# Layer 1's attention on VectorE: the maxima of the scores before the step's weight split, the reciprocal of the sums before the branch read

## The chip, the cores and the metric

The kernel runs on one core of a Trainium2 chip. The metric is the device time of one execution in microseconds. Before the change it is 1315.0 us, the median of three runs (1313.83 to 1315.97).

## The reference

A two-layer diffusion backbone in fp32 for 256 latent and 256 context tokens of width 1024. Each layer normalises and modulates the tokens and projects them once; the columns of that projection feed an attention, a convolution branch (31 taps over positions), a short gated convolution and a Fourier branch, and four gates. Each branch is projected to 1024 channels, multiplied by its sigmoid gate, summed and projected again; a gated MLP follows. In layer 1 only the 256 latent tokens go through the branches. Its attention, cut to what matters:

```
s = q @ k.T * 64 ** -0.5          # 256 latent queries, 512 keys (own and context), 8 heads, band mask
m = maximum(max(s), sink)
p = exp(s - m)
y = (p / (sum(p) + exp(sink - m))) @ v
```

## The kernel before

**Weights in two halves.** Every fp32 product is made of three matmuls: w_hi with the high part of the data, w_hi with its low part, w_lo with its high part (L516 to L518, in `product`). Weights stream through four raw buffers. For each step, ScalarE copies the raw weights of the step three ahead to w_hi (`head`, L940) and VectorE subtracts to get w_lo (`rest`, L1227). A raw buffer is loaded again when VectorE's split of it is done. TensorE begins a step when the split of its weights is done.

**Places.** In layer 1 the eight "fn" steps are places 0 to 7, the eight "sc" steps places 8 to 15, and the first "at" steps go on from 16. A step of a place computes a gate (24 matmuls of 128x256 from h) and a mix (6 matmuls from the branch's data); VectorE's branch read (L1537, which signals `evac`) multiplies the two.

**The attention between the steps.** It is cut into eight batches (two query blocks, four pairs of heads). Batch k begins at place 2k, so it takes a pair of places. Helpers say what falls where: `at_place(layer, place, late)` gives the batch of an even offset, `halves_at` the batch and the half.

- TensorE, at place 2k, between the gate and the mix: the scores of batch k (L758 and the band mask, L764), after both exponentials of batch k-1 (they share the score banks); the values of batch k-2 (L786); the transposes of batch k-1's first half (L774). At place 2k+1: the transposes of its second half.
- VectorE: `peak(k)` at place 2k (two reductions to maxima, L1484, and two operations on two columns, L1487 and L1490); `attended_rest(k-2)` at place 2k (L1504); `weight_sum(k)` at place 2k+1 (the sum, L1496, and its reciprocal, L1498).
- ScalarE: `weigh(k, half)`, the exponential, at places 2k and 2k+1 (L1064); `share(k)`, both halves scaled by the reciprocal, at the start of place 2k+2 (L1075), ahead of that place's `head`; `turned`, the copy of the transposed weights, at places 2k+2 and 2k+3 (L1083).

**The order on each engine** is the order in which its program is written; all waiting is by semaphores. In a place, ScalarE runs share, head, the gate's tanh (L1118), attended, turned, weigh. VectorE runs `rest`, a conv tap (L1471), `peak` (even places), `attended_rest`, a second conv tap, the branch read, and then `weight_sum` (odd places). GpSimd runs the conv taps of the other channel half on its own (L478 and L480, until 978.8 us) and later the sums of the branches (L486).

`early_table` (L945) is a one-column activation into a scratch column, by which ScalarE loads its next function table early; the scratch column is a column of `small`, in which the maxima of even batches are kept.

Of the kernel before, what the change touches and what calls it, by code (L numbers as in the profile page):

```python
# [160 lines left out]
def program(nc, io):  # L161
    ctx = ExitStack()
    with ctx:
# [3 lines left out]
        def at(name, shape, dt, offset):  # L167
            return nc.alloc_sbuf_tensor_at(name, [P] + shape, dt, offset=offset)

        def place(name, shape, dt=F32):  # L170
            size = 4
            for s in shape:
                size *= s
            offset = top[0]
            top[0] += -(-size // 32) * 32
            return at(name, shape, dt, offset)
# [37 lines left out]
        small = place("small", [2, 6, 2])  # L214
        band = at("band", [3, P], BF16, top[0])
        top[0] += 2 * 3 * P
        root_col = place("root_col", [NT // P])
        ada_part = place("ada_part", [2, P * KD // 32])
        assert top[0] <= nc.sbuf_usable_end, (top[0], nc.sbuf_usable_end)

# [32 lines left out]
        def mix_bank(layer, n):  # L253
            return psB[1] if layer and n % 2 else psB[3]
# [4 lines left out]
        def score_bank(layer, half):  # L259
            return psA[2 - 2 * layer + half]  # L260
# [40 lines left out]
        def V(name, i):  # L301
            return vec[:, VEC[name] + i:VEC[name] + i + 1]
# [15 lines left out]
        def branch_sum(layer, o):  # L318

            return X[:, o, 0:NT] if layer == 0 else X[:, o, SEQ:NT]  # L320
# [22 lines left out]
        def at_place(layer, place, late):  # L343

            count, every = NB[layer], 1 + layer
            k, odd = divmod(place - late, every)
            return k if odd == 0 and 0 <= k < count else None
# [11 lines left out]
        def wide(layer, k):  # L359

            return (4 if batches(layer)[k][0] == 0 else 2) * P
# [568 lines left out]
        def _(act):  # L930
# [13 lines left out]

            def early_table(func):  # L945

                act.activation(small[:, 0, 0, 0:1], V("one", 0), func)

            def square(count, o, T, direct, before):

# [268 lines left out]
        def _(dve):  # L1219
            def rest(st, tiles):  # L1220

                if st.i is None and st.n + AHEAD >= TOTAL:
                    return
                s = (st.n + AHEAD) % SLOTS
                r, _ = st.filled("w", AHEAD)
                dve.wait_ge(head_done, st.up(st.n + AHEAD + 1))
                dve.tensor_tensor(w_lo[:, s, 0:tiles * P], raw[:, r, 0:tiles * P],  # L1227
                                  w_hi[:, s, 0:tiles * P].bitcast(F32), ALU.subtract).then_inc(rest_done, 1)

            def size(st, name):  # L1230
                return SIZE[START[name]] if st.i is not None else SIZE[(st.n + AHEAD) % PER_LAYER]
# [162 lines left out]
            for layer in range(DEPTH):  # L1394
# [67 lines left out]
                def conv_tap(j):  # L1462

                    w = V("conf_w", TAPS * layer + j)
                    src, dst = glu[:, 0, 0:S, j:j + SEQ], both(acc[:, 0, 0:T], T)
                    if j == 0:
                        dve.wait_ge(evac, n0 + LEN["in"])
                        op = dve.tensor_scalar(dst, src, w, V("conf_b", 2 * layer), ALU.mult, ALU.add)
                    else:
                        dve.wait_ge(tap, CONF_K * layer + j)  # L1470
                        op = dve.scalar_tensor_tensor(dst, src, w, dst, ALU.mult, ALU.add)  # L1471
                    op.then_inc(tap, 1)
# [4 lines left out]
                def peak(k):  # L1477
                    _, _, t = un[k]
                    b = b0 + k
                    sm = small[:, b % 2, :, :]  # L1480
                    sink = nsink[:, layer * N_HEADS + t:layer * N_HEADS + t + 5:4]
                    for half in range(2):
                        dve.wait_ge(s_mm, 2 * b + half + 1)
                        dve.tensor_reduce(sm[:, 0, half:half + 1], score_bank(layer, half)[:, 0:wide(layer, k)], AX.X,  # L1484
                                          ALU.max).then_inc(negm, 1)
                    dve.wait_ge(negm, 4 * b + 2)
                    dve.scalar_tensor_tensor(sm[:, 1, :], sm[:, 0, :], -HEAD ** -0.5, sink, ALU.mult, ALU.min)\  # L1487
                        .then_inc(negm, 1)
                    dve.wait_ge(negm, 4 * b + 3)
                    dve.tensor_tensor(sm[:, 5, :], sm[:, 1, :], sink, ALU.subtract).then_inc(negm, 1)  # L1490

                def weight_sum(k):
                    b = b0 + k
                    sm = small[:, b % 2, :, :]
                    dve.wait_ge(expd, 3 * b + 3)
                    dve.tensor_tensor(sm[:, 4, :], sm[:, 2, :], sm[:, 3, :], ALU.add).then_inc(den, 1)  # L1496
                    dve.wait_ge(den, 2 * b + 1)
                    dve.reciprocal(sm[:, 4, :], sm[:, 4, :]).then_inc(den, 1)  # L1498

                def attended_rest(k):  # L1500
                    s, qi, t = un[k]
                    c0 = SEQ * s + P * qi
                    dve.wait_ge(o_head, b0 + k + 1)
                    dve.tensor_tensor(y_lo[:, 4 + t, c0:c0 + P], out_bank[:, 0:P],  # L1504
                                      y_hi[:, 4 + t, c0:c0 + P].bitcast(F32), ALU.subtract).then_inc(o_rest, 1)

                def branch(name, b, place=None):
                    def step(st):
                        rest(st, size(st, name))
                        if name == "cf" and st.idx > 0:  # L1510
                            merged_rest(st.idx - 1)
                        o = st.idx
                        if place is not None:
                            if 2 * place < CONF_K:
                                conv_tap(2 * place)
                            k = at_place(layer, place, 0)
                            if k is not None:
                                peak(k)
                            k = at_place(layer, place, LATE[layer]["value"])
                            if k is not None:  # L1520
                                attended_rest(k)
                            if 2 * place + 1 < CONF_K:
                                conv_tap(2 * place + 1)
                            if layer == 0:
                                weight_sum(place)
                        dve.wait_ge(sigd, 34 * layer + 2 + 8 * b + o + 1)
                        dve.wait_ge(chunk_done, st.n + 1)
                        sg = (sig if b == 3 else gsig)[st.n % 2][:, 0:T]
                        ps = (psB[st.n % 2] if b == 3 else mix_bank(layer, st.n))[:, 0:T]
                        if b == 0:  # L1530
                            t = branch_sum(layer, o)
                        else:
                            t = (tmp if b == 3 else gtmp)[st.n % 2][:, 0:T]
                            g = 8 * (b - 1) + o
                            if g >= 2:
                                dve.wait_ge(m_sum, 24 * layer + g - (o > 0))
                        dve.scalar_tensor_tensor(t, sg, 1.0, ps, ALU.add, ALU.mult).then_inc(evac, 1)  # L1537
                        if place is not None and layer and place % 2:
                            weight_sum(place // 2)
                        if name == "fn" and o in (5, 6):  # L1540
                            c = o - 5
                            dve.wait_ge(sc_head, 2 * layer + c + 1)
                            dve.tensor_tensor(y_lo[:, 2 + c, 0:T], pc[:, c, 0:T],
                                              y_hi[:, 2 + c, 0:T].bitcast(F32), ALU.subtract).then_inc(sc_rest, 1)
                        if layer == 0:
                            ada_behind(st)
                    return step

                def merged_rest(o):
                    dve.wait_ge(m_head, 8 * layer + o + 1)  # L1550
                    dve.scalar_tensor_tensor(mg_lo[:, o, 0:T], branch_sum(layer, o), 0.5,
                                             mg_hi[:, o, 0:T].bitcast(F32), ALU.mult, ALU.subtract).then_inc(m_rest, 1)
# [6 lines left out]
                for idx in range(LEN["at"]):  # L1559
# [3 lines left out]
                    k = at_place(layer, 16 + idx, LATE[layer]["value"])  # L1563
# [244 lines left out]
```

## Time and profile before

| | |
|---|---|
| median of three runs | 1315.0 us |
| the profiled execution | 1315.8 us, its span 1314.0 us |
| TensorE busy | 1264.8 us, 96% of the span |
| VectorE busy | 885.3 us, 67% |
| ScalarE busy | 550.2 us, 42% |
| GpSimd busy | 292.9 us, 22% |
| granted TensorE clock, mean | 0.990 |
| layer 1's places 0 to 18 | 928 to 1022 us of the span, about |

Shares are of the span from the first to the last instruction. Busy time of an engine counts its instructions; time in which it waits for a semaphore is idle. In a row of the timeline the number in brackets is the idle time of the engine just before the instruction, and the arrow names what ended it.

### The profile page before, as it was taken

To read this page: it belongs to the slowest core of one execution; us is meant where nothing else is said; L and a number is where in the kernel's file an instruction comes from. 1 tells how busy PE (TensorE), PEld (TensorE's weight loads), DVE (VectorE), ACT (ScalarE), POOL (GpSimd) and SP (SyncE) were. 2 spreads that over 40 slices of the span, in tenths; PEclk is the share of its full clock that TensorE was granted. 3 is DMA by queue.
4 is the path that set the end of the run, shared out by engine and by line. 5 is a ranking of instruction groups with operands and counts; after the bars stand their busy time and mean duration, and the time that the engine had idled before them with its cause. 6 is when DMAs were issued, how large, how long until landed. Compare 5 with 4: busy or idle time off the path is not lost.

```text
span 1314.0 us, 19888 instructions
## 1 busy us (share of the span) xinstructions
PE 1264.8 (96%) x7661; PEld 1094.7 (83%) x7661; DVE 885.3 (67%) x1203; ACT 550.2 (42%) x870; POOL 292.9 (22%) x247
## 2 busy tenths in 40 slices
PE   5999999999999999999999999999989998999997
PEld 3788777777788788888888888889878998999997
DVE  4698678652799767662889674476676667665654
ACT  4322355554423344331223332244556545653543
POOL 0003699110233001111001110003771130210210
PEclk9999999999999999999999999999999998999999
DMA  9465311212366415562646664135333554664561
GB/s 372 159 221 199 120 61 62 73 64 81 116 201 228 131 62 177 192 216 77 204 161 196 198 214 131 62 113 179 106 117 98 183 171 129 193 221 136 185 209 33
DMA packets 50339, 198.76 MB, mean 151 GB/s; under 512 B 5584, under 2 KB 6992, under 8 KB 49104
## 3 DMA queue, kind: packets, MB, share of 16 engines
q1 hardware_dynamic: 50256, 197.62, 45.4%
q8 instruction: 56, 0.92, 0.3%
q14 instruction: 27, 0.22, 0.1%
HBM read 196.55 MB, written 1.05 MB: 150 GB/s over the span
## 4 chain that ended last, share of the span: by engine, by line
PE 85%; DVE 9%; ACT 4%; issue 2%; DMA 1%; SPq 0%; ACTq 0%; DVEq 0%
PE psA L516 25%; PE psA L517 24%; PE psA L518 24%; DVE w_lo L1227 2%; ACT w_hi L940 2%; PE psB L518 2%; PE psB L516 2%; PE psB L517 2%; DVE acc L1471 2%; DVE small L1484 1%; PE psA L758 1%; PE psB L786 1%; PE psB L774 1%; PE psB L689 1%; PE psB L537 1%
## 5 line engine op out<-in xcount | busy, mean ns | idle before, releaser
L516 PE MATMUL psA<-h_hi,w_hi 128*128 128x256 f32 (+1 forms) x1544 | 525.4, 340 | 10.6 <-DVE h_lo L1347 4.9
L517 PE MATMUL psA<-h_lo,w_hi 128*128 128x256 f32 (+1 forms) x1544 | 518.3, 336 | 0.0
L518 PE MATMUL psA<-h_hi,w_lo 128*128 128x256 f32 (+1 forms) x1544 | 518.1, 336 | 0.0
L1227 DVE TENSOR_TENSOR w_lo<-raw,w_hi 128x1024 fp32r<-128x1024 f32 (+2 forms) x244 | 336.5, 1379 | 123.2 <-ACT w_hi L940 123.0
L940 ACT ACTIVATE w_hi<-raw 128x1024 fp32r<-128x1024 f32 (+2 forms) x244 | 277.0, 1138 | 303.1 <-PE psA L518 239.7
L516 PEld LDWEIGHTS psA<-h_hi,w_hi 128*128 128x128 f32 x1544 | 296.8, 192 | 44.4 <-issue 9.5
L518 PEld LDWEIGHTS psA<-h_hi,w_lo 128*128 128x128 f32 x1544 | 296.9, 192 | 29.1
L517 PEld LDWEIGHTS psA<-h_lo,w_hi 128*128 128x128 f32 x1544 | 297.1, 192 | 27.9 <-issue 0.2
L505 POOL TENSOR_TENSOR hid_lo<-sig,hid_hi 128x512 f32 (+3 forms) x44 | 67.7, 1539 | 477.6 <-ACT hid_hi L1191 477.6
L1248 DVE SCALAR_TENSOR_TENSOR ada_sum<-raw,csil,ada_sum 128x1024 f32<-128x1024 f32 x112 | 156.0, 1424 | 0.0
L516 PE MATMUL psA<-hid_hi,w_hi 128*128 128x256 f32 (+1 forms) x352 | 117.5, 334 | 2.1 <-DVE sig L1668 2.0
L518 PE MATMUL psA<-hid_hi,w_lo 128*128 128x256 f32 (+1 forms) x352 | 117.2, 333 | 0.0
L517 PE MATMUL psA<-hid_lo,w_hi 128*128 128x256 f32 (+1 forms) x352 | 117.1, 333 | 0.0
L1632 DVE SCALAR_TENSOR_TENSOR X<-psA,mod,X 128x256 f32<-128x256 f32 x55 | 25.2, 482 | 84.8 <-PE psA L518 84.8
L1658 DVE SCALAR_TENSOR_TENSOR tmp<-psA,vec,tmp 128x510 f32<-128x510 f32 (+1 forms) x44 | 27.1, 616 | 73.1 <-ACT tmp L1202 73.0
L480 POOL TENSOR_TENSOR acc<-acc,sqb 128x512 f32<-128x512 f32 (+1 forms) x60 | 75.1, 1252 | 5.0
L1202 ACT ACTIVATE tmp<-psA,vec 128x512 f32<-128x512 f32 (+1 forms) x44 | 29.5, 671 | 110.4 <-PE psA L518 110.4
L516 PEld LDWEIGHTS psA<-hid_hi,w_hi 128*128 128x128 f32 x352 | 66.8, 190 | 9.3 <-DVE w_lo L1227 2.9
L518 PEld LDWEIGHTS psA<-hid_hi,w_lo 128*128 128x128 f32 x352 | 66.9, 190 | 6.4
L517 PEld LDWEIGHTS psA<-hid_lo,w_hi 128*128 128x128 f32 x352 | 66.9, 190 | 6.4
L486 POOL TENSOR_TENSOR X<-X,tmp 128x512 f32<-128x512 f32 (+1 forms) x28 | 44.5, 1596 | 100.3 <-DVE tmp L1537 52.8
L486 POOL TENSOR_TENSOR X<-X,gtmp 128x512 f32<-128x512 f32 (+1 forms) x20 | 21.2, 1066 | 138.0 <-DVE gtmp L1537 93.8
(190 smaller groups left out, 1461.3 us busy)
## 6 DMA issues: line engine op xcount, KB each, us to landing
raw<-w_up SPq DMA_DIRECT2D x88, 512.0 KB, 4.3
raw<-w_ada SPq DMA_DIRECT2D x80, 512.0 KB, 3.6
raw<-w_dn SPq DMA_DIRECT2D x32, 704.0 KB, 4.8
raw<-w_in SPq DMA_DIRECT2D x36, 512.0 KB, 4.3
raw<-w_at SPq DMA_DIRECT2D x24, 512.0 KB, 3.5
raw<-w_fn SPq DMA_DIRECT2D x16, 640.0 KB, 3.9
raw<-w_sc SPq DMA_DIRECT2D x16, 640.0 KB, 3.8
raw<-w_cf SPq DMA_DIRECT2D x16, 640.0 KB, 3.9
```

Source lines behind the costliest of these rows:

```text
L480: pool.tensor_tensor(dst, dst, part, ALU.add).then_inc(tap_pool, 1)
L486: pool.tensor_tensor(dst, dst, src[:, 0:T], ALU.add).then_inc(m_sum, 1)
L505: pool.tensor_tensor(dst, sig[b][:, 0:T], src.bitcast(F32), ALU.subtract)\
L516: pe.matmul(out, w0, hi, start=first, stop=False)
L517: pe.matmul(out, w0, lo, start=False, stop=False)
L518: return pe.matmul(out, w1, hi, start=False, stop=last)
L940: act.activation(w_hi[:, s, 0:tiles * P], raw[:, r, 0:tiles * P], ACT.Copy).then_inc(head_done, 1)
L1202: act.activation(tmp[b][:, 0:T], psA[st.slot][:, 0:T], ACT.Identity, bias=Vd("ffn_b", st.up(p0 + pair, 2)), scale=Vd("ffn_w", st.up(3 * (p ...
L1227: dve.tensor_tensor(w_lo[:, s, 0:tiles * P], raw[:, r, 0:tiles * P], w_hi[:, s, 0:tiles * P].bitcast(F32), ALU.subtract).then_inc(rest_don ...
L1248: op = dve.scalar_tensor_tensor(dst, w, c, dst, ALU.mult, ALU.add)
L1471: op = dve.scalar_tensor_tensor(dst, src, w, dst, ALU.mult, ALU.add)
L1658: dve.scalar_tensor_tensor(t3[:, :, 1:SEQ], p3[:, :, 0:SEQ - 1], Vd("ffn_w", st.up(w, 6)), t3[:, :, 1:SEQ], ALU.mult, ALU.add).then_inc(cv, 1)
```

## The change

For layer 1 alone, two calls move within VectorE's order of a place. `peak(k)` goes from behind the first conv tap to the very start of the place, ahead of `rest`. `weight_sum` goes from behind the branch read to between the two conv taps. Layer 0 keeps its order. The scratch column that `early_table` writes becomes a tile of its own, `spare`, because the maxima of the first batch may now be taken at an earlier point. No instruction is added or removed.

```diff
+        spare = place("spare", [1])
...
-                act.activation(small[:, 0, 0, 0:1], V("one", 0), func)
+                act.activation(spare[:, 0:1], V("one", 0), func)
...
                 def branch(name, b, place=None):
                     def step(st):
+                        k = at_place(layer, place, 0) if place is not None else None
+                        if k is not None and layer:
+                            peak(k)
                         rest(st, size(st, name))
...
                             if 2 * place < CONF_K:
                                 conv_tap(2 * place)
-                            k = at_place(layer, place, 0)
-                            if k is not None:
+                            if k is not None and layer == 0:
                                 peak(k)
                             k = at_place(layer, place, LATE[layer]["value"])
                             if k is not None:
                                 attended_rest(k)
+                            if layer and place % 2:
+                                weight_sum(place // 2)
                             if 2 * place + 1 < CONF_K:
                                 conv_tap(2 * place + 1)
...
                         dve.scalar_tensor_tensor(t, sg, 1.0, ps, ALU.add, ALU.mult).then_inc(evac, 1)
-                        if place is not None and layer and place % 2:
-                            weight_sum(place // 2)
```

## Rows read from the trace of the kernel before

**Rows 1.** Page, part 1: busy us (share of the span) and instructions of each engine

```profile
PE 1264.8 (96%) x7661; PEld 1094.7 (83%) x7661; DVE 885.3 (67%) x1203; ACT 550.2 (42%) x870; POOL 292.9 (22%) x247
```

**Rows 2.** Windows: us, engines' busy time (instructions), clock, DMA share, GB/s

```profile
928.00:998.00 70.00, 64.41 (x540) 56.70 (x539) 50.31 (x89) 40.90 (x84) 48.56 (x62) 1.00 0.32 106
...
998.00:1022.00 24.00, 23.54 (x211) 21.69 (x211) 15.40 (x32) 16.01 (x33) 2.93 (x4) 1.00 0.37 114
...
950.30:962.70 12.40, 10.65 (x93) 9.34 (x92) 9.99 (x16) 7.50 (x18) 11.13 (x15) 1.00 0.35 108
```

**Rows 3.** Waits of TensorE, 926 to 1022 us: total, times, longest

```profile
PE psA L758 <- ACT prob L1064: 3.1, 5, 1.0
PE psB L774 <- ACT prob L1075: 2.5, 3, 1.1
PE psB L774 <- ACT probT L1083: 0.5, 1, 0.5
```

**Rows 4.** Waits of ScalarE, the same stretch

```profile
ACT prob L1064 <- DVE small L1487: 21.3, 8, 2.9
ACT prob L1075 <- DVE small L1498: 14.8, 8, 2.8
```

**Rows 5.** Waits of VectorE, the same stretch

```profile
DVE w_lo L1227 <- ACT w_hi L940: 25.7, 17, 2.6
```

**Rows 6.** Chain of waits: start, us, what

```profile
949.18 1.17 ACT w_hi L940
...
952.74 1.21 DVE small L1484 x2
```

**Rows 7.** Timeline of TensorE: start, us, what, [idle before <- releaser]

```profile
935.70 1.13 PE L758 MATMUL psA<-k,q 64*128 64x512 f32 x4
...
945.64 1.13 PE L758 MATMUL psA<-k,q 64*128 64x512 f32 x4 [0.44 <-ACT prob L1064]
...
957.90 1.13 PE L758 MATMUL psA<-k,q 64*128 64x512 f32 x4 [1.02 <-ACT prob L1064]
...
993.34 1.13 PE L758 MATMUL psA<-k,q 64*128 64x512 f32 x4 [0.22 <-ACT prob L1064]
...
994.62 1.09 PE L786 MATMUL psB<-probT,v 128*64 128x128 f32 x16
...
1003.99 1.13 PE L758 MATMUL psA<-k,q 64*128 64x512 f32 x4
```

**Rows 8.** Timeline of VectorE

```profile
924.90 1.51 DVE L1227 TENSOR_TENSOR w_lo<-raw,w_hi 128x1280 fp32r<-128x1280 f32 x1 [0.86 <-ACT w_hi L940]
...
928.51 1.29 DVE L1484 TENSOR_REDUCE small<-psA 128x1 f32<-128x512 f32 x2 [1.68 <-PE psA L764]
...
947.64 0.17 DVE L1498 RECIPROCAL small<-small 128x2 f32<-128x2 f32 x1
...
950.37 1.49 DVE L1227 TENSOR_TENSOR w_lo<-raw,w_hi 128x1280 fp32r<-128x1280 f32 x1 [2.56 <-ACT w_hi L940]
951.78 0.96 DVE L1471 SCALAR_TENSOR_TENSOR acc<-glu,vec,acc 128x256 f32<-128x256 f32 x1
952.67 1.28 DVE L1484 TENSOR_REDUCE small<-psA 128x1 f32<-128x512 f32 x2
...
954.42 0.28 DVE L1504 TENSOR_TENSOR y_lo<-psB,y_hi 128x128 fp32r<-128x128 f32 x1
...
955.52 0.41 DVE L1537 SCALAR_TENSOR_TENSOR X<-gsig,psB 128x256 f32<-128x256 f32 x1
...
968.58 2.02 DVE L1227 TENSOR_TENSOR w_lo<-raw,w_hi 128x1280 fp32r<-128x1280 f32 x1
```

**Rows 9.** Timeline of ScalarE, batch 0

```profile
936.14 1.33 ACT L1075 ACTIVATE prob<-prob,small 128x512 f32<-128x512 f32 x2 [2.79 <-DVE small L1498]
```

**Rows 10.** Timeline of GpSimd

```profile
949.02 0.74 POOL L480 TENSOR_TENSOR acc<-acc,sqb 128x256 f32<-128x256 f32 x1
...
950.42 2.04 POOL L480 TENSOR_TENSOR acc<-acc,sqb 128x256 f32<-128x256 f32 x1
```

## The prediction

> **What bounds the kernel now.** I read the busy shares first: TensorE is busy for 96% of the span [rows 1], so only its idle time can be won. The windows come next, to see where it idles near the change. From 928 to 998 us it is busy 64.41 of 70 us, and from 998 to 1022 us 23.54 of 24 us [rows 2]; that is 5.59 + 0.46 = 6.05 us idle, at a granted clock of 1.00 throughout. These two windows are places 0 to 18 of layer 1, where the attention is spread over the branch steps. The waits name the releasers of that idle time: TensorE's scores wait 3.1 us for ScalarE's exponentials and its transposes 2.5 and 0.5 us for ScalarE's scaled weights and copy [rows 3], together 6.1 us, so the whole idle time is here. But ScalarE itself waits 21.3 us for VectorE's maxima (L1487) and 14.8 us for its reciprocal (L1498) [rows 4], and VectorE waits 25.7 us for ScalarE's half of the weight split (L940) [rows 5]. Two engines that are busy for 50.31 and 40.90 of the 70 us [rows 2] wait for each other. The chain of waits shows it in one pair of places: ScalarE's w_hi at 949.18, then VectorE's maxima at 952.74 [rows 6], though the scores had started at 945.64 [rows 7] and took 1.28 us.
>
> One batch takes a pair of places (even, odd). The scores start at 945.64, 957.90, 993.34 and 1003.99 [rows 7]: a pair with waits lasts 12.26 us, the last one 10.65, and that last one begins and ends its scores without a wait worth more than 0.22. I take 10.65 as TensorE's own length of a pair. Two more starts, 969.98 and 982.47, lie between the second and the third of these, and give 12.08, 12.49 and 10.87; over 10.65 the four are 1.61 + 1.43 + 1.84 + 0.22 = 5.10 us, and with 0.44 ahead of 945.64 and the 0.46 idle at the end 6.00, which is the idle time of the windows again. The most that the change can win in this way is therefore 6.05 us, unless TensorE's own work shrinks, and no edit touches that.
>
> **Part 1, the maxima ahead of the split (eight even places).** No instruction is added or removed. Before, VectorE ends its reciprocal at 947.81, stands 2.56 us for w_hi, runs the split from 950.37, a conv tap from 951.78, and reduces from 952.67 [rows 8]. The scores of this batch had ended at 945.64 + 1.28 = 946.92, so moved ahead the maxima start at 947.8, inside a gap that is 2.56 us long. They take 954.42 − 952.67, about 1.75 us (the next row begins at 954.42; two reductions and two small operations), so the gap holds them and the split doesn't start later. What was serial, split 1.41 + tap 0.89 = 2.30 us, goes out of the way of ScalarE's exponential. What is late next is ScalarE's own order: w_hi, tanh, the copy of the transposed weights, then the exponential.
>
> Behind the moved maxima stand, on VectorE, this place's split, its taps and the release of the place's banks (evac). Once pairs are at 10.65 us, the scores come later relative to VectorE, so it will stand at the maxima. Laid out from the start of the scores as 0: scores ready at 1.3, maxima to 3.1, split to 4.6, two taps, the y_lo part and evac (at 0.89, 0.89, 0.21 and 0.33) to 6.95, the odd split from 7.3 to 8.75. The split is for three places on: TensorE needs that of the even place about 14 us after 0. Each place has 3.8 us of products ((10.65 − 1.28 − 1.05 − 0.75)/2, the values and transposes taken off), evac is read two places on, at about 13.3, and the raw buffer that the split frees is loaded for a place four on; the queue of loads therefore gets its slot at most as late as the split moves. Their cost is nothing while the margins of some 6 to 9 us stand; without them it would be the overrun itself.
>
> Place 0 is the exception. Its split ran at 924.90 and the maxima at 928.51 [rows 8]; now it stands behind them and runs at 930.4 to 931.9, and its two taps and its evac follow some 2.7 us later than they did. The split is wanted by place 3 at about 938. The odd split, the tap and the weight sum that follow end at about 936.3, where scaling began at 936.14 before [rows 9]. I charge 0.2 us for it, with 0 and 1.5 us as ends.
>
> **Part 2, the reciprocal ahead of the branch read (eight odd places).** The weight sum takes 0.35 us and moves ahead of a tap (0.89 under contention) and of the 0.41 us branch read [rows 8], so it comes 1.2 us earlier in VectorE's order. It adds a wait: with it now stand the second tap, the branch read and the next maxima behind ScalarE's second exponential. In the layout the odd gate is ready at 6.4, tanh, copy and exponential (0.3, 0.5, 0.9) end near 8.4, while VectorE comes to the weight sum at 9.6 after its split and tap: the wait is over already. The reciprocal is there at 10.0, which is 0.65 us before the next scores; before the change it came at 947.8 − 945.64 = 2.2 us after them. The first half is scaled 0.7 us later, and TensorE's transpose wants it 1.28 + 1.02 us after the scores start [rows 7]: it is there 2.2 us early. So the waits on the scaled weights (2.5) go, and those on the exponentials (3.1) as well, whose second half is ready at 8.4 against 10.65. For the copy (0.5) the scaling of the last batch sits about 1 us earlier, so it should go too. The next things that end are VectorE's round of 9.99 us of busy time in a pair [rows 2] and TensorE's 10.65.
>
> Part 3, the scratch column of the table load: same count and shape, off any path, 0 us (from −0.2 to 0.2).
>
> **Contention, weighed.** GpSimd runs its own conv taps beside VectorE until 978.8: an addition takes 0.74 us alone and 2.04 us when it starts within 0.05 us of VectorE's split [rows 10], and VectorE's split takes 2.02 us instead of 1.49 in one place [rows 8]. The windows' 9.99 us already hold such cases. The moved split can fall on other GpSimd operations. The Trainium skill (SBUF — State Buffer, Who interferes with whom) says that a VectorE instruction with two SBUF inputs and a GpSimd instruction that reads SBUF exclude each other, and that the first to issue holds the ports to its end; the 2.04 agrees with that, and by it every one of the splits could be unlucky. That is the second case below, worked out from rows.
>
> **Sum.** 6.1 us of waits, less 0.2 for place 0 and 0.2 left over, is 5.7. The profiled execution took 1315.8 us (span 1314.0 and 1.8 around it), so 1310.1; it lies 0.8 above the median of 1315.0, on which scale it is 1309.3. Later stages wait on TensorE's progress, so the gain should pass through to the end.
>
> **Rivals.** (A) VectorE becomes the bound under contention. Both splits at 2.02 add 1.06, and half of the taps going from 0.5 to 0.96 add 0.3: 9.99 + 1.36 = 11.35 us a pair, 0.7 over TensorE's. In three or four pairs that gives 2.1 to 2.8 back: 1311.8. For it: 9.99 leaves only 0.66 us. Against: unlucky overlaps are in the 9.99 already, and a GpSimd that is held up starts later.
> (B) A wait takes the place of another: the scores are on time, but the reciprocal, with the even place's split and taps between it and the maxima, comes later than 1.6 us after the next scores, and the transposes wait. At 2.0 us in each of seven pairs this is 7 × 0.4 = 2.8 us new on top of the 2.5 that stay, against 3.1 + 0.5 won: 0.8 us net, 1314.2. For it: the split no longer uses the gap but follows the maxima. Against: 2.2 us of margin in the layout.
> (C) Slower: VectorE, in order, stands at the maxima for scores and at the weight sum for exponentials with splits behind, and what it stands adds to its round: 9.99 + 1.4 + 1.5 = 12.9 us a pair while GpSimd's taps run. Against 9.94 (935.70 to 945.64), 12.26, 12.08 and 12.49 before, that is +4.9 us, less 0.7 won afterwards: 1319.2. It decides from a round of 12.3. Against: VectorE stands only where it is early, and no wait of TensorE hangs on the end of the same pair's round.
>
> **From cases to numbers.** Forecast 0.68, (A) 0.14, (B) 0.11, (C) 0.07. A change of 0.2% (2.6 us) is about what can be told from none. The forecast and (A) are faster: 0.82; (B) is the same: 0.11; (C) slower: 0.07. The range goes from 1307.4 (the cap of 6.05 and 1.5 us of spread between runs) to 1313.8, over (A) and up to (B).
>
> **What would show it.** Right: scores some 10.65 us apart from the second batch on; ScalarE's waits for L1487 near zero but for that of place 0, and under 5 us in all; the reciprocal between two taps, ahead of the scores of the next batch; TensorE's idle time from 928 us on under 0.7 us; VectorE's new wait at L1484 for the scores, up to 1.5 us in each pair. Wrong: pairs of 11.3 us with VectorE busy throughout (A), transposes waiting for L1075 (B), pairs over 12.3 (C), or a gain that is given back after place 18, seen as idle time of TensorE behind 1016 us that was not there.

## The result, and the profile after

The changed kernel takes 1308.12 us, the median of five runs (1307.57 to 1309.83), against 1315.0 before. The ratio is 0.9949, with a 95% interval of 0.9936 to 0.9962: 6.9 us faster, and by the interval 5 to 8.4. 5.7 were forecast. The profiled execution took 1307.6 us, its span 1305.7, 8.3 less than before. The line numbers are one higher than before (L1485 for L1484), and three to five higher in and behind the branch step.

I split the spans at TensorE's first scores of layer 1 and at the last batch's values. Before they lie at 927.18 and 1021.49 us, after at 925.91 and 1013.42.

| stretch | before | after | less by |
|---|---|---|---|
| start of the span to the first scores | 927.18 | 925.91 | 1.27 |
| first scores to the last values | 94.31 | 87.51 | 6.80 |
| last values to the end | 292.51 | 292.28 | 0.23 |

All that was moved lies in the middle stretch, called "the stretch" from here on. The 1.27 us ahead of it are no effect: in the profiles below the first scores start anywhere from 924.6 to 928.1 us, whatever the order. The windows of the new kernel, the same as in [rows 2], show TensorE without a gap; behind the length of a window stand the busy times of TensorE's matmuls, its weight loads, VectorE, ScalarE and GpSimd:

```profile
928.00:998.00 70.00, 70.00 (x589) 62.10 (x589) 59.40 (x105) 48.45 (x96) 54.08 (x60) 1.00 0.38 123
998.00:1022.00 24.00, 24.00 (x222) 23.19 (x221) 13.27 (x21) 13.25 (x25) 2.39 (x2) 1.00 0.42 132
```

TensorE's waits of [rows 3] have no successor between 926 and 1016 us. The scores (start, us, what) are evenly spaced, where [rows 7] had 12.26:

```profile
943.99 1.13 PE L759 MATMUL psA<-k,q 64*128 64x512 f32 x4
...
954.50 1.13 PE L759 MATMUL psA<-k,q 64*128 64x512 f32 x4
...
975.53 1.13 PE L759 MATMUL psA<-k,q 64*128 64x512 f32 x4
```

Each pair from the third scores on is 10.51 us. The other engines' waits (line waited for: total, times, longest; 926 to 1016 us, since the last values now come 8 us earlier) show what was exchanged; VectorE's of [rows 5] and ScalarE's of [rows 4] answer to these:

```profile
DVE small L1485 <- PE psA L765: 13.5, 7, 4.5
DVE w_lo L1228 <- ACT w_hi L941: 5.6, 3, 2.3
DVE small L1497 <- ACT small L1070: 1.6, 2, 0.9
```

```profile
ACT prob L1076 <- DVE small L1499: 10.1, 8, 2.9
ACT gsig L1119 <- PE psA L519: 9.5, 7, 2.4
...
ACT prob L1065 <- DVE small L1488: 2.8, 1, 2.8
```

VectorE's standing for w_hi fell from 25.7 to 5.6 us. It now stands at the maxima for TensorE, 13.5 us, and ScalarE stands for TensorE's gates, 9.5 us. That is how a stretch looks in which TensorE leads: the others wait for it. ScalarE's 21.3 us for the maxima are 2.8, in place 0 alone.

One pair of VectorE's timeline, places 4 and 5, which answers to [rows 8]:

```profile
945.32 1.29 DVE L1485 TENSOR_REDUCE small<-psA 128x1 f32<-128x512 f32 x2 [0.46 <-PE psA L765]
...
947.12 1.49 DVE L1228 TENSOR_TENSOR w_lo<-raw,w_hi 128x1280 fp32r<-128x1280 f32 x1
...
951.68 0.96 DVE L1472 SCALAR_TENSOR_TENSOR acc<-glu,vec,acc 128x256 f32<-128x256 f32 x1
...
952.75 0.17 DVE L1499 RECIPROCAL small<-small 128x2 f32<-128x2 f32 x1
...
955.83 1.29 DVE L1485 TENSOR_REDUCE small<-psA 128x1 f32<-128x512 f32 x2 [1.66 <-PE psA L765]
```

The scores started at 943.99; the maxima follow at 945.32 and the reciprocal is there at 952.9, 1.6 us before the next scores, where it came 2.2 us behind them.

### The profile page after: what moved, and what is told of

Its sections match the earlier page's. It is cut to its first block, busy times and chain, and to the rows that moved or that the text cites. A ratio compares the mean times of both kernels' runs of the same rounds, so it can differ in the third digit from the quotient of the medians.

```text
span 1305.7 us, 19888 instructions
## 1 busy us (share of the span) xinstructions
PE 1262.0 (97%) x7661; PEld 1093.7 (84%) x7661; DVE 887.1 (68%) x1203; ACT 552.1 (42%) x870; POOL 298.0 (23%) x247
## 4 chain that ended last, share of the span: by engine, by line
PE 90%; DVE 6%; ACT 2%; issue 1%; DMA 0%; SPq 0%; DVEq 0%; ACTq 0%
PE psA L517 26%; PE psA L518 25%; PE psA L519 25%; PE psB L519 2%; PE psB L517 2%; PE psB L518 2%; PE psB L775 1%; PE psA L759 1%; PE psB L787 1%; DVE acc L1472 1%; DVE w_lo L1228 1%; ACT w_hi L941 1%; PE psB L690 1%; PE psB L538 1%; DVE small L1485 1%
## 5 line engine op out<-in xcount | busy, mean ns | idle before, releaser
L487 POOL TENSOR_TENSOR X<-X,gtmp 128x512 f32<-128x512 f32 (+1 forms) x20 | 25.7, 1293 | 125.3 <-DVE gtmp L1542 80.5
```

The costliest lines, as they stand in the source:

```text
L487: pool.tensor_tensor(dst, dst, src[:, 0:T], ALU.add).then_inc(m_sum, 1)
```

## The experiments

The theory: VectorE and ScalarE stood in one closed round of waits (reciprocal, scaling, w_hi, split, tap, maxima, exponential, w_hi, exponential, reciprocal) that was longer than TensorE's pair of places; either edit shortens the round. The rival: there are two separate waits, and each edit removes its own. The measure that spread elsewhere doesn't blur is the stretch. It is read from one profiled execution of each kernel, and it repeats where the order in it is the same: 94.31 and 94.37 us for the old one, 87.51, 87.50 and 87.55 for the new one. The granted clock is 1.00 over all of it in every profile but one, e_extra4, which is taken up there.

**The scratch tile alone.**

```diff
+        spare = place("spare", [1])
-                act.activation(small[:, 0, 0, 0:1], V("one", 0), func)
+                act.activation(spare[:, 0:1], V("one", 0), func)
```

> Only the scratch column of the table load gets its own tile; the order is that of before. Theory (all of the gain is in the attention's places): no change, 1315.0 within 1 us, scores of layer 1 start at about 927 us and pairs stay at 12.1 to 12.5 us. Rival (the new tile or the moved addresses behind it are worth something, since the first scores of the changed kernel start 1.27 us earlier than before, ahead of every moved instruction): 1.3 us faster, with the first scores at 925.9.

Measured: 1314.56 against 1315.35 us, ratio 0.9995 (0.9986 to 1.0005), the stretch 94.37 us. No effect of the tile can be seen. But the first scores stood at 925.61, with the order of before, so that time ahead of the stretch varies without any cause in the order.

**The maxima alone.** Against the changed kernel:

```diff
-                            if layer and place % 2:
-                                weight_sum(place // 2)
...
                         dve.scalar_tensor_tensor(t, sg, 1.0, ps, ALU.add, ALU.mult).then_inc(evac, 1)
+                        if place is not None and layer and place % 2:
+                            weight_sum(place // 2)
```

> Maxima ahead of the split as in the changed kernel, weight sum behind the branch read as before. Theory (the gap ahead of the split swallows the maxima, and the round of waits that goes from the reciprocal over scaling, w_hi, split, tap and maxima back to the exponential is cut there): the reciprocal comes at about 0.8 us after the next scores instead of 0.65 ahead of them, the transposes want the scaled half 2.3 us after them, so TensorE does not wait: pairs of 10.5 us and the full gain, 6 to 7 us. Rival (both parts are needed, each removes one of the two waits): the waits on the exponentials go (3.1 us), those on the scaled weights stay (2.5 us), gain 3 to 3.5 us.

Measured: 1308.75 us, ratio 0.9951 (0.9939 to 0.9963), the stretch 88.64 us, 5.67 less than before. The pairs are 10.51 us from the third scores on, as the theory says, but the stretch gives 5.67 where the theory had the full gain, 6 to 7 us. The rest is one wait of TensorE, in place 2 (start, us, what, idle before):

```profile
937.78 0.44 PE L775 MATMUL psB<-mat,prob 128*128 128x128 f32 x2 [1.15 <-ACT prob L1076]
```

This is the batch whose weight sum follows place 0's late split. The rival's 2.5 us of waits in later pairs are not there.

**The weight sum alone.** Against the changed kernel, the maxima go back behind the first tap:

```diff
-                        if k is not None and layer:
-                            peak(k)
...
-                            if k is not None and layer == 0:
+                            if k is not None:
                                 peak(k)
```

> Weight sum between the two taps, maxima behind the first tap as before. Theory (one closed round of waits between VectorE and ScalarE of 12.1 to 12.5 us; the weight sum is 1.2 us earlier in it): pairs of about 11.1 us where they were 12.1 to 12.5, 10.5 at the end, gain 4 to 4.5 us, ScalarE still waiting 2 us and more for L1487 (its line of before) in each pair. Rival (each part removes its own wait of TensorE): only the waits on the scaled weights go, gain 2.5 us.

Measured: 1310.67 us, ratio 0.9962 (0.9949 to 0.9976), the stretch 90.34 us, 3.97 less. Pairs of 11.52, 11.49, 11.30, 10.76 and 10.52 us. Here is what is left of the waits, of TensorE and of ScalarE:

```profile
PE psA L759 <- ACT prob L1065: 2.5, 4, 0.9
```

```profile
ACT prob L1065 <- DVE small L1488: 21.3, 8, 3.3
ACT prob L1076 <- DVE small L1499: 8.9, 8, 1.7
```

The rival gave 2.5 us, and the interval of the ratio excludes less than 3.1. The pairs are 0.4 longer than the 11.1 that I had laid out: the 1.2 us of the move gave 0.6 to 1.2 a pair. The two parts alone add to 9.6 us and together give 6.80. By the rival the two would add up to no more than the whole. They draw on the same round, and TensorE's 10.51 is the floor. By name the rival has it right: here the waits on the scaled weights go and 2.5 us on the exponentials stay, and with the maxima alone it is the other way round. The name of the releaser says who came last, not how much an edit can win.

**The maxima behind the split, ahead of the tap.** Against the changed kernel; the weight sum goes back behind the branch read as well:

```diff
-                        if k is not None and layer:
-                            peak(k)
                         rest(st, size(st, name))
...
+                        if k is not None and layer:
+                            peak(k)
...
-                            if layer and place % 2:
-                                weight_sum(place // 2)
...
                         dve.scalar_tensor_tensor(t, sg, 1.0, ps, ALU.add, ALU.mult).then_inc(evac, 1)
+                        if place is not None and layer and place % 2:
+                            weight_sum(place // 2)
```

> Maxima behind the split and ahead of the first tap, weight sum behind the branch read as before. Theory (what counts is that the maxima use the gap in which VectorE stands for w_hi): the gap stays empty, only the tap (0.7 to 0.9 us) goes out of the round: pairs of about 11.4 us, gain 2.5 to 3.5 us. Rival (anything ahead of the exponential is as good, the split can be paid): the same gain as with the maxima ahead of the split, 6 to 7 us.

Measured: 1312.99 us, ratio 0.998 (0.9966 to 0.9994), the stretch 91.84 us, 2.47 less. Pairs of 11.44, 11.51, 11.39, 11.31 and 10.66. VectorE goes on standing for the split with the maxima ready behind it:

```profile
959.82 0.17 DVE L1499 RECIPROCAL small<-small 128x2 f32<-128x2 f32 x1
...
962.55 1.49 DVE L1228 TENSOR_TENSOR w_lo<-raw,w_hi 128x1280 fp32r<-128x1280 f32 x1 [1.73 <-ACT w_hi L941]
963.96 1.28 DVE L1485 TENSOR_REDUCE small<-psA 128x1 f32<-128x512 f32 x2
```

So of the 5.67 us of the maxima, 3.2 come from passing the split: its gap and its 1.4 us.

**Load on VectorE.** Two reductions of 128x512 behind each batch's maxima of layer 1 (n = 2), then four (n = 4), against the changed kernel. `spare` grows to 64 columns, and nothing reads the results:

```diff
                             peak(k)
+                            for i in range(n):
+                                dve.tensor_reduce(spare[:, 1 + n * k + i:2 + n * k + i], M("pos", 512), AX.X, ALU.max)
```

> The changed kernel with two more reductions of 128x512 behind each batch's maxima on VectorE (0.61 us each from start to start, results unused), so its round in a pair is 1.2 us longer. Theory (TensorE is the bound with 1.4 us of margin at the tightest transposes, 3 us at the others): 0 to 1.2 us slower than the changed kernel, 1308 to 1309.5. Rival (A, VectorE is at its limit already): the four pairs beside GpSimd's taps grow by 0.7 to 1.2 us each, 3 to 5 us slower than the changed kernel.

> The changed kernel with four more reductions per batch, VectorE's round 2.45 us longer: own rounds of 11.6, 12.5, 11.3 and 12.4 us in the pairs beside GpSimd's taps against TensorE's 10.5. Theory (the round beyond the margin is paid in full): 4 to 5.5 us slower than the changed kernel, 1312 to 1313.6, with waits of TensorE for L1076's scaled weights. Rival (C, standing times add to the round): pairs over 13.5 us and slower than before, over 1317.

Measured: with two 1308.74 us, ratio 0.9947 (0.9923 to 0.9971), the stretch 88.76 us, 1.25 more than the changed kernel; with four 1311.86 us, ratio 0.9973 (0.9959 to 0.9988), the stretch 92.19 us, 4.68 more. Nearly all of it sits between the second and the third scores, 10.80 and 13.67 us where the changed kernel has 9.56, and not in the pairs beside GpSimd's taps, as rival (A) would have it. With two, the size is at the upper end of what the theory gave. With four it looks like the theory's 4 to 5.5 us, but part of it is something else. TensorE's long wait for the first batch's scaled weights, 2.63 us,

```profile
937.41 0.66 PE L775 MATMUL psB<-mat,prob 128*128 128x128 f32 x4 [2.63 <-ACT prob L1076]
```

is followed, from 938.2 to 941.6 us, by a granted clock at the lower of its two levels, 1.2 GHz; the column behind the five busy times is the clock's share:

```profile
939.00:941.00 2.00, 2.00 (x12) 2.00 (x11) 1.98 (x5) 2.00 (x6) 1.69 (x3) 0.50 0.00 0
```

The 16 steps from one matmul to the next in these 3.4 us take 0.21 us each instead of 0.12, which makes about 1.5 us (an estimate). Without it the load of four costs some 3.2 us, less than the theory gave.

With two reductions the first batch, not the pairs beside GpSimd's taps, is where the margin ends. That led to the next two.

**The same load, place 0 in the order of before.** Split and first tap of place 0 ahead of its maxima (and of the added reductions); all else as in the two kernels above:

```diff
-                        if k is not None and layer:
+                        if k is not None and layer and place:
...
-                            if k is not None and layer == 0:
+                            if k is not None and (layer == 0 or place == 0):
```

> Two more reductions per batch as in e_extra2 (results unused), but place 0 keeps the order of before, split and first tap ahead of the maxima; weight sums as in the changed kernel. From the first scores to the last values e_extra2 took 88.76 us against 87.51, all of the 1.25 between the second and the third scores. Theory (place 0's late split sets the tight place, the rest has margin): 87.5 to 87.7 us from the first scores to the last values, pairs of 10.5 from the third scores on, 9.5 to 9.7 between the second and the third. Rival (two reductions are more than VectorE has room for): 88.5 us or more.

> The same with four more reductions per batch. e_extra4 took 92.19 us from the first scores to the last values, 4.1 of its 4.7 us more between the second and the third scores. Theory (2.45 us less 1.2 us of margin won in place 0, and some lateness handed on): 88.5 to 90.5 us. Rival (the load itself is over the limit and the loss only moves to later pairs): 91.5 us or more.

Measured, one execution each: the stretch is 87.29 us with two and 90.61 with four, at a clock of 1.00. With two TensorE waits for no other engine, and the second to the third scores take 9.34 us, 0.22 less than in the changed kernel without any load; both are a little under the 87.5 and 9.5 us that the theory gave at least. So the late split of place 0 costs the changed kernel 0.2 us and takes away its margin at batch 0. With four the result is 0.1 over the upper end of what the theory gave, and the later pairs now are 10.91, 10.87, 11.41 and 11.90 us. They hold 3.05 of the 3.10 us over the changed kernel, which is as much as the 3.2 us that four reductions cost before, the clock taken off. So with four the rival has it right in kind, though its 91.5 us was not reached: the loss moved to the later pairs, and the 1.6 us that the order in place 0 saved are mostly what the clock had cost. That is the limit of VectorE's round that rival (A) spoke of. It lies between 1.2 us more a pair, which costs nothing, and 2.45.

**GpSimd's taps left out of the kernel before.** All but the first of its conv taps in layer 1 are left out:

```diff
-                for j in range(CONF_K):
+                for j in range(CONF_K if layer == 0 else 1):
...
-                            .then_inc(tap_pool, 2)
+                            .then_inc(tap_pool, POOL_STEPS if layer else 2)
```

> The kernel before without GpSimd's conv taps of layer 1 but the first (that part of the convolution is left out). Theory (contention with GpSimd doubles VectorE's taps from 0.48 to 0.96 us, and these stand in the round of waits): pairs of 10.7 to 11.0 us from the third batch on, as in the last pairs of before, gain about 4 us over before. Rival (the long taps are VectorE's own, from their place behind the split): pairs stay at 12.1 to 12.5 us, no gain.

Measured: 1308.97 us, ratio 0.9941 (0.9922 to 0.9961), the stretch 89.01 us, 5.3 less, and pairs of 10.51 to 10.87. Its taps and splits on VectorE, 926 to 1016 us (ns min/median/max):

```profile
L1471 DVE SCALAR_TENSOR_TENSOR acc<-glu,vec,acc x30: 472/477/485, 928.2 to 1006.4; 128x256 f32<-128x256 f32 x30
```

```profile
L1227 DVE TENSOR_TENSOR w_lo<-raw,w_hi x18: 1224/1491/1493, 930.1 to 1014.8; 128x1280 fp32r<-128x1280 f32 x12, 128x1024 fp32r<-128x1024 f32 x6
```

With GpSimd's taps beside them the 30 taps took 473 to 976 ns, and a split up to 2.02 us [rows 8]. Most of what made the old round longer than TensorE's pair was this contention, more of it than I had thought (5.3 us, not 4); the pairs are still up to 0.36 us over 10.51. VectorE goes on standing for w_hi (29.1 us from 926 to 1016 us) and ScalarE for the maxima (19.3 us): two engines can wait for each other at no cost, as long as their round is no longer than TensorE's pair. By the Trainium skill (SBUF — State Buffer, Who interferes with whom) the order of issue decides which of the two engines stands. The trace of before agrees with that: GpSimd's addition at 950.42 us came 0.05 us behind a split and took 2.04 us while the split took its 1.49 [rows 8, 10], and the split of 2.02 us at 968.58 [rows 8] came 0.16 us behind a GpSimd addition that took 0.83.

**Layer 0 in the new order.** Its maxima go ahead of the split too:

```diff
-                        if k is not None and layer:
+                        if k is not None:
                             peak(k)
...
-                            if k is not None and layer == 0:
-                                peak(k)
```

> The changed kernel with the maxima ahead of the split in layer 0 too. TensorE waits there 0.9 us for scaled weights and 0.5 us for exponentials in all. Theory (TensorE is busy there anyway): 0 to 1.4 us faster than the changed kernel, 1306.7 to 1308.1. Rival (the split and the work for the modulation behind the maxima come late in the short steps): 1 to 4 us slower than the changed kernel.

Measured: 1308.63 against 1315.9 us, ratio 0.9937 (0.9921 to 0.9953). Layer 0's attention, from its first scores to its last values, took 153.38 us against 155.05 in the changed kernel. I put this together with the old order in place 0 of layer 1 and timed the changed kernel beside it.

```diff
-                        if k is not None and layer:
+                        if k is not None and not (layer and place == 0):
...
-                            if k is not None and layer == 0:
+                            if k is not None and layer and place == 0:
                                 peak(k)
```

> The changed kernel with the maxima ahead of the split in layer 0 too, and in place 0 of layer 1 the order of before. Theory: the 1.67 us that layer 0's attention was shorter with the maxima ahead of the split (153.38 against 155.05 us from the first scores to the last values) come again, and 0.1 us in place 2 of layer 1; 1.5 to 1.8 us faster than the changed kernel timed beside it, which five rounds can only just tell from nothing. Rival (the 1.67 is spread between executions): the same time as the changed kernel.

> The changed kernel again, to be timed beside the one with layer 0 changed too. 6.5 to 7 us faster than before; 87.5 us from the first scores of layer 1 to the last values, as the first time.

Measured: 1306.8 us (1306.42 to 1309.94), ratio 0.9941 (0.9927 to 0.9954), against 1309.01 us (1306.76 to 1309.99), ratio 0.9952 (0.9939 to 0.9966), for the changed kernel. That one is 6.1 us faster than the kernel before, timed beside it at 1315.12 us, where I had expected 6.5 to 7. It has the stretch of the first time, 87.50 us; the kernel with both edits has 87.29. But the changed kernel's layer 0 took 153.23 us this time, as short as with the new order (153.40). In the twelve profiles of layer 0's old order it is either 153.2 to 153.6 (five) or 155.0 to 155.4 (seven), so the 1.67 us can be spread between executions. The version with both edits has the lowest median of all, the intervals overlap, and whether layer 0's new order keeps the long state away stays open: both of its profiles are short, which is too few.

## Why the prediction was right

**What bounds it.** Right. TensorE's own pair was the floor, the round between VectorE and ScalarE what held it, and all of TensorE's idle time in these windows went. The sentence that the change can win at most 6.05 us was wrong: the stretch got 6.80 shorter.

**Part 1, the maxima.** Right in mechanism: they run as soon as the scores are there and the split behind them has margin. Alone they give 5.67 of the 6.80 us. Place 0 was charged 0.2 us; with that place in the old order (e_both, and e_extra2_place0 with load) the second to the third scores take 9.34 us instead of 9.56, which is 0.22.

**Part 2, the weight sum.** The forecast treated it as taking away the waits on scaled weights. With the maxima moved those are nearly gone without it: it adds 1.13 us, all in place 2. The laid-out 0.65 us ahead of the next scores came out as −0.2, 1.6, 0 and 1.7 us in the four pairs beside GpSimd's taps, from the second scores on. In the pair of the 0 both splits took over 2 us, in those of the 1.6 and 1.7 no more than 1.49, so I put the spread down to contention; no run was made for it. The added wait for the exponentials is there in the last two pairs, 1.6 us in all, and nobody waits for it.

**The sum.** This is what was mis-sized, by 1.1 us: 5.7 for the stretch's 6.80. The forecast took the time to be won from TensorE's idle time as its matmul rows show it, and TensorE's own pair as 10.65 us; the pair is 10.51. Measured on starts of scores the gain is 0.38 for the first two pairs, (12.26 + 12.08 + 12.49 + 10.87 + 10.65) − 5 × 10.51 = 5.80 for the next five, and 0.63 behind the last scores, in places 16 and 17, where 0.46 was seen; 6.8 in all. Each pair was longer than its floor by 0.12 to 0.17 us more than its idle time shows, whether two stops are shown in it, one, or none. The missing part stands in the rows of the weight loads, which the forecast did not read. Here are those of a pair with a wait and of the last one, of 10.65 us, which it took as TensorE's own length:

```profile
957.90 0.30 PEld L758 LDWEIGHTS psA<-k,q 64*128 64x128 f32 x4 [1.22 <-ACT prob L1064]
...
1003.99 0.30 PEld L758 LDWEIGHTS psA<-k,q 64*128 64x128 f32 x4 [0.20 <-ACT prob L1064]
```

The matmuls behind these two loads show 1.02 us of idle time and none. In the stretch of the new kernel no load of the scores' weights waits for the exponentials.

**Rivals.** (A) did not come: the changed kernel's pairs beside GpSimd's taps are 10.51, with VectorE standing 0.5 to 2.4 us at the maxima in each from the third batch on, where the forecast gave up to 1.5; by the load runs 2.45 us more a pair brings it and 1.2 does not. (B) did not: no transpose waits. (C) did not either: with VectorE's round lengthened by 2.45 us, its standing shrinks instead of adding up (the waits at the maxima go from 13.5 to 5.2 us, of which 4.5 are place 0's in both), and the kernel stays faster than before.

**Passing through.** Right: behind the last values 292.28 us against 292.51.

## What to carry to other kernels

When two engines that are not busy each wait for the other, follow one round of their waits and compare its length with the bottleneck's own period; only the excess can be won, and several edits to the same round share it. Move into a gap the work that is ready before the gap ends, ahead of the instruction that the in-order engine stands at, and check what that instruction feeds: here it had three places of margin, except in the first place, where the pipeline had no gap yet. Take the period from starts of the same instruction, not from idle times, and look at what the weight loads wait for before a pair is called free of waits. When a load or a delay is put in, look at the granted clock before its cost is put down to the delay alone.

## What the hardware showed that I had not expected

The idle time ahead of a matmul row understates how long TensorE stood. At the scores of the old kernel the weight loads waited 0.20 us longer than the matmul rows show, 1.22 against 1.02 and 0.20 against none, and the pairs were 0.12 to 0.17 us longer than floor and idle time together. The ends of matmuls are modelled in these profiles, so the time in between can look busy.

One idle time of 2.63 us of TensorE, with four reductions a batch, was followed by 3.4 us at a granted clock of 0.50. The waits of the old kernel, up to 1.15 us each, were not: its clock stays at 1.00 from 926 to 1022 us.

Layer 0's attention takes one of two times with the same order of work, 153.2 to 153.6 or 155.0 to 155.4 us. Between the changed kernel's two profiles 1.5 of the 1.8 us sit in two spacings of scores, 10.32 and 9.96 us against 9.71 and 9.07, where TensorE waits 0.54 and 0.64 us for ScalarE in the long one and not in the short one. No run here tells why ScalarE is late there.
